# Twelve of the sixteen gate units of a layer by a 2x2x2 seven-product scheme, in a two-block transformer kernel on one core

## What is computed

```python
p_swa, p_rwkv, p_fox, p_dsa, p_gate = split_cols(x @ w_in, IN_GROUPS)
...
gates = jax.nn.sigmoid(p_gate.reshape(B, S, N_BRANCHES, D_MODEL) + gate_bias)
...
for i, (o, w) in enumerate(zip((o_swa, o_rwkv, o_fox, o_dsa), w_rows)):
    merged = merged + gates[:, :, i] * (o @ w)
return merged @ w_out
```

## Time and profile before

| | us |
|---|---|
| Median of 3 runs (lowest, highest) | 2172.64 (2172.41, 2173.16) |
| The profiled execution | 2173.13 |
| Its span (first to last instruction) | 2171.4 |
| TensorE busy in it | 2092.4 (96%) |
| VectorE busy | 875.6 (40%) |
| ScalarE busy | 374.7 (17%) |
| GpSimd busy | 74.5 (3%) |

### The profile page before, as it was taken

One profiled execution on the slowest core, in us unless ns is written; L12 is line 12 of the kernel. 1 busy time (PEld: TensorE's weight loads), 2 busy tenths in 40 slices (PEclk: granted clock), 3 DMA queues, 4 the chain that ended last, 5 costly groups with the idle time before them and its releaser, 6 DMA issues.

```text
span 2171.4 us, 37454 instructions
## 1 busy us (share of the span) xinstructions
PE 2092.4 (96%) x16270; PEld 1553.5 (72%) x16270; DVE 875.6 (40%) x1693; ACT 374.7 (17%) x899; POOL 74.5 (3%) x180
## 2 busy tenths in 40 slices
PE   8998999999999989999999999999999999999998
PEld 8786786887788867866653554388687768868786
DVE  1414525677734154242010000135566754454443
ACT  1312240000013122401010000133300012431000
POOL 3000000010000000020000000000000010000000
PEclk9999899999999998998999999999999999999999
DMA  9334234598563342327999999962568754333452
GB/s 261 97 98 153 90 126 151 182 322 277 194 197 98 97 160 78 126 79 235 348 312 377 345 347 326 315 212 97 176 238 291 265 182 151 98 117 120 154 174 97
DMA packets 333831, 421.44 MB, mean 194 GB/s; under 512 B 27222, under 2 KB 282148, under 8 KB 333668
## 3 DMA queue, kind: packets, MB, share of 16 engines
q1 hardware_dynamic: 312464, 352.96, 50.3%
q0 software_dynamic: 13408, 50.66, 6.6%
q10 hardware_dynamic: 7796, 15.43, 2.0%
HBM read 417.90 MB, written 1.05 MB: 193 GB/s over the span
## 4 chain that ended last, share of the span: by engine, by line
PE 84%; DMA 6%; DVE 4%; ACT 3%; ACTq 1%; issue 1%; SPq 0%; DVEq 0%
PE psum L1295 15%; PE psum L1327 13%; PE psum L1434 11%; PE psum L1302 9%; PE psum L1312 9%; PE psum L1494 5%; DMA ring<-in_w_up 4%; PE psum L1958 3%; PE psum L1565 3%; PE psum L1740 2%; PE psum L1339 2%; DMA ring<-in_ffn_w 2%; ACTq L653 1%; PE psum L1423 1%; PE psum L1507 1%
## 5 line engine op out<-in xcount | busy, mean ns | idle before, releaser
L1295 PE MATMUL psum<-xT,ring 128*128 128x256 f32 x1600 | 373.7, 394 | 6.8 <-ACT small L779 4.1
L1295 PEld LDWEIGHTS psum<-xT,ring 128*128 128x128 f32 x1600 | 312.1, 197 | 63.1 <-issue 7.0
L1312 PE MATMUL psum<-ring,arena 128*128 128x512 f32 x528 | 232.1, 593 | 0.0
L1302 PE MATMUL psum<-ring,xT 128*128 128x256 f32 (+2 forms) x960 | 201.1, 367 | 2.8 <-DVE arena L2466 2.1
L1302 PEld LDWEIGHTS psum<-ring,xT 128*128 128x128 f32 x960 | 170.6, 190 | 29.4 <-DVE arena L2466 2.7
L1312 PEld LDWEIGHTS psum<-ring,arena 128*128 128x128 f32 x528 | 97.9, 190 | 111.8 <-issue 111.6
L2145 DVE SCALAR_TENSOR_TENSOR arena<-arena,cond 128x512 f32<-128x512 f32 x168 | 126.2, 751 | 5.5
L1327 PEld LDWEIGHTS psum<-xT,ring 128*128 128x128 f32 x960 | 112.8, 194 | 20.7 <-issue 20.7
L1434 PE MATMUL psum<-ring,arena 128*32 128x256 f32 x2304 | 126.8, 379 | 0.7 <-DVE arena L2299 0.7
L1327 PE MATMUL psum<-oT,arena 128*128 128x128 f32 x960 | 117.4, 275 | 5.9 <-DVE arena L2160 5.8
L1327 PE MATMUL psum<-xT,ring 128*128 128x128 f32 x960 | 114.1, 278 | 6.0 <-DMA ring<-in_w_up 3.5
(11 more groups left out here) (414 smaller groups left out, 2518.4 us busy)
## 6 DMA issues: line engine op xcount, KB each, us to landing
ring<-in_w_in SPq DMA_DIRECT2D x80, 1024.0 KB, 5.5
ring<-in_exp_w SPq DMA_DIRECT2D x312, 256.0 KB, 6.2
arena<-in_w_mod POOLq DMA_DIRECT2D x48, 1024.0 KB, 9.2
ring<-in_ffn_w SPq DMA_DIRECT2D x33, 1024.0 KB, 7.3
arena<-in_exp_w SPq DMA_DIRECT2D x120, 256.0 KB, 7.1
ring<-in_w_gate SPq DMA_DIRECT2D x22, 1024.0 KB, 7.6
ring<-in_w_up SPq DMA_DIRECT2D x22, 1024.0 KB, 10.1
ring<-in_w_down SPq DMA_DIRECT2D x22, 1024.0 KB, 5.0
```

What stands on the lines that cost most here:

```text
L1295: ins = pe.matmul(dst, w[:, k * 256 + c0:k * 256 + c0 + m], act_t[:, k, :], start=(k == 0), stop=(k == KT - 1))
L1302: ins = pe.matmul(dst, xT[:, k, t * P:t * P + P], w[:, k * 256 + c0:k * 256 + c0 + n], start=(k == 0), stop=(k == KT - 1))
L1312: ins = pe.matmul(psum[:, 4 + 2 * t + h, :], gT[:, s % 2, f * 256 + t * P:f * 256 + t * P + P], w2[:, f * D + h * 512:f * D + h * 512 + 51 ...
```

## The change

Gate units are joined in pairs: `PAIRS` holds the first gate unit of each of six pairs per layer (0, 2, 6, 8, 10, 12), so units 4, 5, 14 and 15 stay as they were. A pair's two units a and b, and the tokens, are each cut in 2 x 2 quarters (rows 0-511 and 512-1023; a and b; tokens 0-127 and 128-255), and four quarter results come from seven products of 8 matmuls with 128 token columns instead of eight.

- TensorE (`pair_products`): job q = 0, 1, 2 has two products, q = 3 has one. Jobs 0 and 1 replace the pair's first fill, jobs 2 and 3 the second. Pairs 0 and 1 (level loop and chunk loop) take banks 6 and 7 in turn; pairs 2 to 5 (attention) take bank 7 for every job, one job at the fill's old place and one behind `weigh`. A job waits until the job before it in its bank is joined.
- VectorE: token sums `xsum1` once per layer (four adds of 128x512) behind the BT products, in the space of `rows`; the joins (`join_pair`): 1, 2, 3 and 1 adds of 128x256 for q = 0 to 3. In the attention the join of the odd job opens the next iteration and the join of the even job closes its own.
- ScalarE: one plain copy of 128x256 per pair; the gate bias moves from the fill's copy into the sigmoid, which becomes four operations of 128x256 per output tile.
- GpSimd (`pair_sums`): four adds of 128x1024 per pair, with waits for the units and for TensorE's jobs.
- `wb_first` has rows 0 to 5 and `wb_last` rows 6 to 9; the load of `ln1` moves behind the sigmoids.

```diff
+PAIRS = (0, 2, 6, 8, 10, 12)
...
-        wb_first = view(7, D, at=gate_at - 7 * D)
+        gate_sum2 = view(2, 2, 256, at=gate_at - 7 * D)
+        wb_first = view(6, D, at=gate_at - 6 * D)
         top[0] = 0
-        wb_last = view(3, D)
+        wb_last = view(4, D)
...
+        pair_sum1 = [quarter(0, 6), quarter(0, 4), quarter(0, 6), quarter(2, 6), quarter(0, 6), quarter(2, 6)]
+        pair_sum2 = [quarter(2, 6), quarter(2, 4)] + [gate_sum2] * 4
+        xsum1 = rows[:].rearrange("p a b -> p (a b)").rearrange("p (i k t) -> p i k t", i=4, k=4)
...
+        def pair_bank(p, q):
+            return (6, 7)[q % 2] if p < 2 else 7
...
+            def pair_sums(l, p):
+
+                ua, ub = pair_units(l, p)
+                for u in (ua, ub):
+                    pool.wait_ge(*ready("slot%d" % ring_place[u], "unit", *u))
+                (a_lo, a_hi), (b_lo, b_hi) = halves(ring_place[ua]), halves(ring_place[ub])
+                if p == 0:
+                    pool.wait_ge(*(ready("pe_job", "par") if l == 0 else ready("pe_job", "mod_columns", 0)))
+                if p >= 4:
+                    pool.wait_ge(*ready("pe_job", "pair", l, p - 2, 2))
+                step(pool.tensor_tensor(pair_sum1[p], b_lo, b_hi, ALU.add))
+                step(pool.tensor_tensor(b_lo, a_lo, b_lo, ALU.subtract))
+                if p >= 3:
+                    pool.wait_ge(*ready("pe_job", "pair", l, p - 1, 1))
+                step(pool.tensor_tensor(pair_sum2[p], pair_sum1[p], a_lo, ALU.subtract), "pair_sum2", l, p)
+                pool.wait_ge(*ready("pe_job", "pair", l, p, 0))
+                step(pool.tensor_tensor(a_hi, a_hi, pair_sum2[p], ALU.subtract), "pair_sum4", l, p)
+
             for b in range(N_BARRIERS):
+                for p in (range(0, 2), range(2, len(PAIRS)))[b % BARRIERS_1]:
+                    pair_sums(b // BARRIERS_1, p)
                 barrier()
...
+                    if pair_of(j):
+                        p, half = pair_of(j)
+                        if half == 0:
+                            act.wait_ge(*ready("pe_job", "pair", l, p, 0))
+                            step(act.copy(pair_out(p, 0, 1), two(psum[:, pair_bank(p, 0), 0:256])), "pair", l, p)
+                        continue
...
-                        for i in range(2):
-                            c = 2 * cp + i
-                            step(act.activation(zb[:, b, c, :], bank[:, i * 256:i * 256 + 256],
-                                                ACT.Identity, bias=prm(l, "gate_b", b * KT + c)), "filled", l, j)
+                        step(act.copy(zb[:, b, 2 * cp:2 * cp + 2, :], two(bank)), "filled", l, j)
...
-                load_rows(l, a["ln_g"][l, 0], a["ln_b"][l, 0], "ln1", l)
...
-                    step(act.activation(zb[:, :, c, :], zb[:, :, c, :], ACT.Sigmoid), "sig", l, c)
+                    for b in range(4):
+                        step(act.activation(zb[:, b, c, :], zb[:, b, c, :], ACT.Sigmoid,
+                                            bias=prm(l, "gate_b", b * KT + c)), "sig", l, c)
+                load_rows(l, a["ln_g"][l, 0], a["ln_b"][l, 0], "ln1", l)
...
+            def pair_products(l, p, q):
...
+                bank = pair_bank(p, q)
+                if bank in fill_in:
+                    pe.wait_ge(*ready(*fill_in[bank]))
...
+                if q == 0:
+                    pair_product(bank, 0, a_lo, x11)
+                    ins = pair_product(bank, 1, a_hi, x21)
+                elif q == 1:
+                    pe.wait_ge(*ready("dve", "xsums1", l))
+                    pe.wait_ge(*ready("pool", "pair_sum2", l, p))
+                    pair_product(bank, 0, pair_sum2[p], xsum1[:, 1])
+                    ins = pair_product(bank, 1, b_lo, xsum1[:, 2])
+                elif q == 2:
+                    pair_product(bank, 0, pair_sum1[p], xsum1[:, 0])
+                    pe.wait_ge(*ready("pool", "pair_sum4", l, p))
+                    ins = pair_product(bank, 1, a_hi, x22)
+                else:
+                    ins = pair_product(bank, 0, b_hi, xsum1[:, 3])
+                job(ins, "pair", l, p, q)
+                if q >= 2:
+                    used(*(ua, ub)[q - 2])
+                fill_in[bank] = ("dve", "pair", l, p, q)
...
-                    if i in G[7]:
+                    joint = i in G[7] and pair_of(filled[0] % FILLS)
+                    if joint:
+                        pair_products(l, joint[0], 2 * joint[1])
+                    elif i in G[7]:
                         fill(l, 1, (7,))
...
                     if i >= 3:
                         weigh(l, i - 3, UNITS1[i - 3])
+                    if joint:
+                        pair_products(l, joint[0], 2 * joint[1] + 1)
+                        filled[0] += 1
...
+            def join_pair(l, p, q):
+
+                lower, upper = [two(psum[:, pair_bank(p, q), 256 * i:256 * i + 256]) for i in range(2)]
+                c11, c12, c21, c22 = [pair_out(p, i // 2, i % 2) for i in range(4)]
+                dve.wait_ge(*(ready("act", "pair", l, p) if q == 0 else ready("pe_job", "pair", l, p, q)))
+                if q == 0:
+                    step(dve.tensor_tensor(c11, c12, upper, ALU.add), "pair", l, p, q)
+                elif q == 1:
+                    step(dve.tensor_tensor(c12, c12, lower, ALU.add))
+                    step(dve.tensor_tensor(c21, c12, upper, ALU.add), "pair", l, p, q)
+                elif q == 2:
+                    free(dve.tensor_tensor(c22, c21, lower, ALU.add))
+                    step(dve.tensor_tensor(c12, c12, lower, ALU.add))
+                    step(dve.tensor_tensor(c12, c12, upper, ALU.add), "pair", l, p, q)
+                else:
+                    step(dve.tensor_tensor(c21, c21, lower, ALU.add), "pair", l, p, q)
...
             def attention(l):
                 n = len(UNITS1)
                 for i in range(n + 4):
+                    if 1 <= i < 9:
+                        join_pair(l, 2 + (i - 1) // 2, 2 * ((i - 1) % 2) + 1)
                     if i < n:
                         scores_in(l, i, UNITS1[i])
...
                     if 1 <= i < n + 1:
                         probs(l, i - 1, UNITS1[i - 1])
+                    if i < 8:
+                        join_pair(l, 2 + i // 2, 2 * (i % 2))
...
+                token_sums1(l)
                 for lv in range(1, 6):
+                    if lv in (3, 4):
+                        for q in (2 * (lv - 3), 2 * (lv - 3) + 1):
+                            join_pair(l, 0, q)
...
+                    if c < 2:
+                        for q in (2 * c, 2 * c + 1):
+                            join_pair(l, 1, q)
```

More of the change, by code:

```diff
@@ L943, in _ @@
                         fill(l, G[8], (0, 1))
-                    act.wait_ge(*ready("act", "filled", l, len(FILL_IN) + 4 * (c // 2) + 3))
-                    step(act.activation(zb[:, :, c, :], zb[:, :, c, :], ACT.Sigmoid), "sig", l, c)
+                    for g in range(4 * (c // 2), 4 * (c // 2) + 4):
+                        j = g + len(FILL_IN)
+                        if pair_of(j) is None:
+                            act.wait_ge(*ready("act", "filled", l, j))
+                        elif g % 2:
+                            act.wait_ge(*ready("dve", "pair", l, pair_of(j)[0], 3))
+                    for b in range(4):
+                        step(act.activation(zb[:, b, c, :], zb[:, b, c, :], ACT.Sigmoid,
+                                            bias=prm(l, "gate_b", b * KT + c)), "sig", l, c)
+                load_rows(l, a["ln_g"][l, 0], a["ln_b"][l, 0], "ln1", l)
                 if l == 0:
@@ L1269, in fill @@
                     filled[0] += 1
+                    if pair_of(j):
+                        p, half = pair_of(j)
+                        for q in (2 * half, 2 * half + 1):
+                            pair_products(l, p, q)
+                        continue
                     bank = banks[j % len(banks)]
                     if bank in fill_in:
-                        pe.wait_ge(*ready("act", "filled", l, fill_in[bank]))
+                        pe.wait_ge(*ready(*fill_in[bank]))
                     key = ("in", l, FILL_IN[j]) if j < len(FILL_IN) else ("gate", l, *gate_place(j - len(FILL_IN)))
@@ L1287, in fill, with pair_product @@
                     used(*key)
-                    fill_in[bank] = j
+                    fill_in[bank] = ("act", "filled", l, j)
+            def pair_product(bank, half, weights, tokens):
+                for f in range(2):
+                    dst = psum[:, bank, half * 256 + f * P:half * 256 + f * P + P]
+                    for k in range(4):
+                        ins = pe.matmul(dst, weights[:, k // 2, k % 2, f * P:f * P + P], tokens[:, k, :],
+                                        start=(k == 0), stop=(k == 3))
+                return ins
+            def pair_products(l, p, q):
+                x11, x12, x21, x22 = [xT[:, 4 * (i // 2):4 * (i // 2) + 4, P * (i % 2):P * (i % 2) + P]
```

(22 more changed lines are left out.)

19 lines of the change are left out of this document (16 added, 3 removed).

## The result

The changed kernel takes **2246.09 us** (median of 4 runs, 2243.02 to 2250.82), the kernel before 2172.52 (4 runs on the same chip): ratio **1.035**, 95% interval 1.033 to 1.037, so 73.6 us slower. The forecast was 2233, range 2193 to 2254. The profiled execution took 2246.02 (span 2244.3), 72.9 more than that of before.

A forecast was written before the change was run, and what follows sets the result against it. TensorE was taken as the bound (84% of the chain), VectorE close behind in attention. Terms 29.4 + 16 + 16 + 6 + 1.2 - 8.2 - 0.5 = +59.9 on 2173.1 gave 2233 us, range 2193 to 2254.

The forecast's parts named there:

- The sign: Whole kernel: slower by over 0.2%, chance 0.90; same 0.03, faster 0.07.
- rival (1): VectorE's and GpSimd's operations don't hold each other up: terms of 22 fall away, 2211 us; chance 0.2.
- rivals (2) to (5): Clock stays up, 2217 (0.1); neither, 2195 (0.08); odd jobs don't wait, faster (0.07); gain and waits cancel within 0.2% (0.03).
- Order, +29.4: Attention: TensorE's jobs in bank 7 wait for VectorE's joins in iterations 0 to 3; net +14.7 us per layer.
- two pairs give 2 x 1.7 back: Attention, iterations 4 to 7: without `choose`, two pairs return 2 x 1.7 us, less four waits, 1.4.
- Granted clock, +16: Attention: idle time ahead of odd jobs lowers TensorE's clock, 8 us per layer; bounds 0 and 2 x 14.
- Hold-up in the attention, +16: GpSimd's weight sums hold VectorE's operations on two SBUF operands, +1.39 us per meeting, 8 per layer; bounds 0 and 30 per layer.
- Pair 0's sums, +6: Ahead of the level loop, GpSimd's first adds delay Bh and kh, which TensorE needs: 3 us per layer.
- Level and chunk loops, -8.2: Pairs 0 and 1: 1.75 us saved per pair plus two ScalarE copies of 0.3, 4.1 per layer.
- ln rows, -0.5: Start of kernel: two ln-row issues leave ScalarE's queue ahead of copies TensorE awaits; at least -0.5 us once.
- w_branch, +1.2: Branch matmuls: late rows are 2 MB instead of 1.5, 0.6 us late per layer; bounds 0 and 4.
- Nothing: Token sums hide under a fill, sigmoids under branch matmuls: no cost; without cover 4 x 0.7 and 2 x 6 us.

The follow-up runs named there:

- two edits together: Changed kernel with even jobs joined straight behind scores_in and GpSimd's attention weight sums left out but for four columns: 2202.4 us.
- once GpSimd was silent: Changed kernel with GpSimd's weight sums of pairs 2 to 5 left out but for four columns, products reading unsummed halves: 2231.0 us.
- the four-pair kernels: Changed kernel with four pairs, the attention's two in iterations 4 to 7, and pair 0's sums late: 2170.0 us; with the first attention sums later, 2163.0.
- the fitted matmuls: Changed kernel with 34, 20, 32 and 18 identity matmuls ahead of the odd jobs of iterations 0 to 3, inside the waits: 2232.1 us.
- the overrunning ones: Changed kernel with 68, 38, 60 and 34 identity matmuls ahead of the odd jobs of iterations 0 to 3, longer than the waits: 2262.7 us.
- the edited kernel: Changed kernel with pair 0's weight sums started only when VectorE has made the token sums: 2237.1 us.
- the run without pairs: Changed kernel with PAIRS = (), so no seven-product units, sums or joins, the rest of the change kept: 2168.2 us.
- the kernel with two pairs: Changed kernel with only the level-loop and chunk-loop pairs, whole fills in the attention and pair 0's sums behind the token sums: 2161.2 us.
- two pairs and seven rows: The two-pair kernel with late sums, and w_branch cut at seven rows again as before the change: 2158.1 us.
- the last four-pair kernel: Four pairs, the attention's two in iterations 4 to 7, with GpSimd's first sums there waiting for the inputs of iteration 2's exps: 2163.0 us.

## Why the prediction was right, and which terms were off

The sign, the mechanism and the place held; rival (1), no hold-up, and rivals (2) to (5) fell with the runs above. The forecast was 13 us low. For the two attentions it had 2 x (14.7 + 8 + 8) = 61.4 us and they took 74.0 more than before, so nearly all of the 13 lies there: 8.0 up to fox's scores, 4.7 behind them. The terms can't be told apart to the us, as two edits together gave 5.3 more than their sum. By its terms:

- **Order, +29.4.** The step is right in iterations 0 to 3: 5.3 us idle in iteration 0 and 4 to 5.5 after it were worked out, 5.3, 5.0, 4.0 and 4.7 measured once GpSimd was silent. That kernel reached fox's scores 61.1 us after the first scores, where order and clock together made 59.5. Wrong was "two pairs give 2 x 1.7 back" for iterations 4 to 7. The step that failed is the price of a product, 1.78 us, read where one product follows another: between other work, jobs took 3.67 to 3.77 for two and 1.98 for one, so **a pair gives 0.9 there, not 1.7**. From fox's scores on the sum has 2.3 us less per layer. At the same granted clock the four-pair kernels have 1.1 less and the changed kernel 0.8 less (layer 1, 67.2 against 68.0, both at 0.87). In layer 0 it took 67.2, 0.9 more than the 66.3 before, at 0.87 where it had been 0.90; the same two levels stand in kernels without pairs there, so this fall isn't shown to come from the change.
- **Granted clock, +16.** Measured 14.0 by the fitted matmuls, with 5.3 us of waits left in layer 0; the overrunning ones make it 9 to 11 per layer. Right in size. But the earlier trace rows, from which I took it, doesn't show the cause: the changed kernel has the same wait of 2.06 us at 55.13, and the 32 passes behind it took 7.17 and not 10.05. What shows it are the odd jobs, at 3.78 behind waits of 4.7 to 11 and at 2.05 where the waits were filled (2.98 behind the 3.4 us left in iteration 0 of layer 0).
- **Hold-up in the attention, +16.** Measured 15.1 in the median, in the profiles 10.8 and 9.9 up to fox's scores, clock included. That the term came out right is partly luck, from parts that were off: an add takes 2.35, not 1.9, and a meeting costs about 2 (2.52 for 0.41), not 1.39; fewer meetings count, since those on the search and on PSUM reads cost nothing. Its place was off too: the largest piece is in iteration 0 (wait 11.0 against 5.3, and 1.9 ahead of the even job), where three adds on the forget-gate chain make VectorE 3.5 us later and two more, on L2809 and L2530, 2.1 each. The rest is iteration 2 (7.9 against 4.0).
- **Pair 0's sums, +6.** Measured 9.0 (2237.1 against 2246.1), in the profile 5.2 idle and 0.9 of clock per layer, 12.2 (that profile of the edited kernel came to this stretch 2.1 late, which the total includes): half to two thirds of it was foreseen. I started them at 92, when I took the weights to land; they started at 86.21 and caught all three adds, and my rule let VectorE lose 1.39 a meeting where it lost 2.0.
- **Level and chunk loops, -8.2.** From the fill at 103.21 to the first scores layer 0 gained 4.0 (0.4 late to 3.6 early), and two pairs against none gave -7.0. The sum is right, the parts less so: the half pairs took 7.34 and 5.56 to the next work (132.89 to 140.23, 143.81 to 149.37), where 7.1 and 5.35 were worked out, so a pair gives 1.3 here and about 1 us of the 4.0 comes from outside the products.
- **ln rows, -0.5.** TensorE's fill began 1.4 earlier, at 45.93, and 4.4 more came with the clock (7.17 where the earlier trace rows has 10.05, 3.62 for 5.15). All thirteen profiles with the late ln rows reach the first matmul with `block_ones` at 72.4 to 75.8, the one of before at 78.67. So this was worth 3 to 6 us, if the single profile of before is typical: too small, and the part that the clock gives was not foreseen.
- **w_branch, +1.2.** The waits are 0.49 and 0.73, as forecast for this kernel; they depend on when TensorE gets there, and were 1.7 in the run without pairs and 2.4 to 2.6 with two or four (both layers).
- **Nothing** for token sums and sigmoids: the run without pairs has all 32 sigmoids and is as fast as before. It has no token sums; they stand in the kernel with two pairs, which gained its 7.0 with them.

The Trainium skill (SBUF — State Buffer, "SBUF: two separate sides") says that the shared port pair goes to whichever engine starts first, for its whole instruction. The rows at 86 to 94 us agree: 2.73, 2.72 and 2.71 for adds of 0.69. The sum should have gone by this rule and by what is left of the GpSimd add at each meeting, 1.8 to 2.1 us in the rows above. The Trainium skill (GPSIMD Engine Reference, "3.1 Elementwise — side-by-side cycle accounting") gives 4497 ns for an add of 2048 float32, half of which, as an estimate, is 2.25 for 1024; the rows have 2.35, and the 1.9 that I took came from a multiplication whose inputs are broadcast.

## What to carry to other kernels

Price a job's result by the place of its consumer in the other engine's list: one bank that is emptied at the end of VectorE's iteration serialises the two engines, and long idle times are paid once more in clock (here some 7 us a layer for 28.6 of waits). Put GpSimd adds of SBUF operands where VectorE searches or reads PSUM, never beside a chain of small instructions: each of those, however small, can cost most of a GpSimd add. Read the price of an instruction group where it will stand, start to start, not where it follows its like. Compare two kernels' stretches at the same granted clock. A scheme that saves 0.9 to 1.3 us per pair pays only where nobody waits for its joins: with two of the six pairs the kernel beat the one before by 0.5%, with all six it lost 3.5%.

## What the runs showed of the hardware

- A VectorE instruction on 128x4 numbers took 0.16 alone and 2.25 beside a GpSimd add of 2.34. One-operand TENSOR_SCALAR from SBUF to SBUF was held too (2.33 for 0.28; 2.20 for 0.17).
- MAX8 and MATCH_REPLACE8 kept their 0.43 and 0.41 beside GpSimd's adds at 216 to 221 us of the last four-pair kernel; the adds that read PSUM kept their 0.42 (140.41 and 140.86 in the changed kernel, beside the add at 139.30), and TENSOR_REDUCE its 1.14 (213.27, beside the add at 212.04).
- GpSimd is held in turn: its add took 2.35 alone and 2.68 in the turns with VectorE.
- The same instructions from fox's scores on ran at a granted clock of 0.90 or 0.87 and took 66.3 or 68.0 us (the kernel before, layers 0 and 1). With two pairs it was 0.90 and 0.87, with two pairs and seven rows 0.87 and 0.90. No run here shows what decides it, and a difference of 1.6 us between two single profiles can be this alone.
